# State-space output products: 128 stationary columns, one PSUM bank per head

## What is computed

```python
dt = softplus(dt_raw + dt_bias)
a_cum = cumsum(dt * -exp(a_log))                      # per head, along the tokens
xdt = xs * dt[..., None]                              # [token, head, 64]
decay = exp(where(causal, a_cum[l] - a_cum[s], -inf))
cb = einsum('ln,sn->ls', cm, bm)
y = einsum('ls,ls,sp->lp', cb, decay, xdt)            # sum over source tokens s
y = y + y_off                                         # chunks before, through a state
y = y + xs * d_skip
y = y * silu(z)
```

## Time and profile before

| what | value |
|---|---|
| median of 3 runs | 4614.47 us |
| the profiled execution | 4616.21 us, span 4614.4 us |
| PE busy | 4007.6 us (87%) |
| PEld busy | 3162.7 us (69%) |
| DVE busy | 2151.2 us (47%) |
| second block of `ssd` | about 206.3 to 345.7 us of the span |
| mean granted clock of PE | 0.893 |

### The profile page before, as it was taken

One profiled execution on the slowest core, in us unless ns is written; L12 is line 12 of the kernel. 1 busy time (PEld: TensorE's weight loads), 2 busy tenths in 40 slices (PEclk: granted clock), 3 DMA queues, 4 the chain that ended last, 5 costly groups with the idle time before them and its releaser, 6 DMA issues. The chain is left out here.

```text
span 4614.4 us, 53647 instructions
## 1 busy us (share of the span) xinstructions
PE 4007.6 (87%) x17473; PEld 3162.7 (69%) x17473; DVE 2151.2 (47%) x4054; ACT 1619.1 (35%) x2537; POOL 1620.4 (35%) x896
## 2 busy tenths in 40 slices
PE   7798758999659998998965988697799888999998
PEld 5436646877424566876764875576699888978886
DVE  1642173320233323311277113313498999378877
ACT  2322253322241223312245111322333688533333
POOL 3103233433210014433443431243267666633221
PEclk9759888999775579999988998898899999999999
DMA  2002102222100012222300231122257699799997
GB/s 89 29 0 87 62 14 80 94 92 72 45 29 0 0 37 91 94 88 65 93 14 19 91 96 32 55 91 68 97 174 250 221 336 332 286 357 361 344 343 246
DMA packets 275082, 573.61 MB, mean 124 GB/s; under 512 B 119777, under 2 KB 156001, under 8 KB 274545
## 3 DMA queue, kind: packets, MB, share of 16 engines
q1 hardware_dynamic: 238080, 437.71, 28.5%
q0 software_dynamic: 36864, 134.23, 8.6%
HBM read 517.33 MB, written 54.53 MB: 124 GB/s over the span
## 5 line engine op out<-in xcount | busy, mean ns | idle before, releaser
L382 PE MATMUL ps<-h_hi,w_hi 128*128 128x512 f32 x1868 | 740.7, 397 | 160.5 <-DVEq L510 73.9
L476 POOL TENSOR_TENSOR w_lo<-ring,w_hi 128x1024 fp32r<-128x1024 f32 (+3 forms) x193 | 462.7, 2398 | 1142.6 <-ACT w_hi L453 1142.6
L383 PE MATMUL ps<-h_lo,w_hi 128*128 128x512 f32 x1868 | 736.5, 394 | 0.0
L384 PE MATMUL ps<-h_hi,w_lo 128*128 128x512 f32 x1868 | 735.5, 394 | 0.0
L382 PEld LDWEIGHTS ps<-h_hi,w_hi 128*128 128x128 f32 x1868 | 356.9, 191 | 249.3 <-DVEq L510 63.7
L453 ACT CAST w_hi<-ring 128x1024 fp32r<-128x1024 f32 (+3 forms) x193 | 202.8, 1051 | 868.5 <-PE ps L384 807.5
L2208 PE MATMUL ps<-h_hi,w_hi 128*128 128x384 f32 (+1 forms) x1152 | 400.9, 348 | 22.9 <-PEq L208 21.6
L2035 ACT CAST w_hi<-ring 128x1024 fp32r<-128x1024 f32 x270 | 282.2, 1045 | 373.7 <-PE ps L384 281.0
L2160 POOL TENSOR_TENSOR w_lo<-ring,w_hi 128x1024 fp32r<-128x1024 f32 x142 | 358.0, 2525 | 152.6 <-ACT w_hi L2035 151.5
L384 PEld LDWEIGHTS ps<-h_hi,w_lo 128*128 128x128 f32 x1868 | 356.4, 191 | 75.9
L383 PEld LDWEIGHTS ps<-h_lo,w_hi 128*128 128x128 f32 x1868 | 357.0, 191 | 73.6
(11 more groups left out here) (365 smaller groups left out, 7773.3 us busy)
## 6 DMA issues: line engine op xcount, KB each, us to landing
ring<-in_expert_u SPq DMA_DIRECT2D x128, 512.0 KB, 4.8
ring<-in_expert_v SPq DMA_DIRECT2D x128, 512.0 KB, 5.7
ring<-in_w_gate_up SPq DMA_DIRECT2D x88, 512.0 KB, 3.7
acts<-expert_gelu SPq DMA_DIRECT2D x128, 192.0 KB
gates<-peer_region SPq DMA_DIRECT2D x48, 512.0 KB, 7.0
peer_region<-acts SPq DMA_DIRECT2D x128, 192.0 KB, 4.7
peer_region<-gates SPq DMA_DIRECT2D x128, 192.0 KB, 5.6
ring<-in_w_down SPq DMA_DIRECT2D x32, 704.0 KB, 4.0
```

What stands on the lines that cost most here:

```text
L382: pe.matmul(out, w_hi, x_hi, start=start, stop=False)
L383: pe.matmul(out, w_hi, x_lo, start=False, stop=False)
L384: return pe.matmul(out, w_lo, x_hi, start=False, stop=stop)
L476: pool.tensor_tensor(half(c.w_lo, s), raw(s), half(c.w_hi, s).bitcast(F32), ALU.subtract).then_inc(c.lo_done.sem, 1)
```

## The change

The output product of a head takes the 128 columns of its whole pair as the stationary operand (`xdt[:, j, 128 (h // 2) : ...]`). Its result has 128 partitions: 64 for its own head, and 64 of the other head's channels under this head's weights, which nobody reads. Each head now sums in a bank of its own, in turn 2, 3, 5, 6 (`sum_banks`). `pair(k)` reads the lower 64 partitions of the even head's bank and the upper 64 of the odd head's, with two instructions where one stood. `c_ready` counts two for a pair, and PE waits for it at the first step of every head from the fourth on, not of even heads only. Number and order of PE's products are the same.

```diff
-        banks = (0, 1, 4)
+        banks, sum_banks = (0, 1, 4), (2, 3, 5, 6)
...
-                    if j == 0 and h % 2 == 0 and h >= 4:
-                        pe.wait_ge(c.c_ready.sem, c.c_ready.at(h // 2 - 1))
+                    if j == 0 and h >= 4:
+                        pe.wait_ge(c.c_ready.sem, c.c_ready.at(2 * (h // 2 - 1)))
                     pe.wait_ge(c.b_ready.sem, c.b_ready.at(n + 1))
-                    p0 = 64 * (h % 2)
-                    mm = pe.matmul(c.ps[p0:p0 + 64, 2 + (h // 2) % 2, j * P:T], xdt[:, j, 64 * h:64 * h + 64],
+                    p0 = P * (h // 2)
+                    mm = pe.matmul(c.ps[:, sum_banks[h % 4], j * P:T], xdt[:, j, p0:p0 + P],
                                    M[:, n % 2, 0:T - j * P], start=j == 0, stop=j == NCH - 1)
...
                     dve.wait_ge(c.d_ready.sem, c.d_ready.at(2 * NCH * (k + 1)))
-                    dve.scalar_tensor_tensor(out[:, k, :], xs(k), c.col("d_skip", k),
-                                             c.ps[:, 2 + k % 2, :], ALU.mult, ALU.add).then_inc(c.c_ready.sem, 1)
-                    dve.wait_ge(c.c_ready.sem, c.c_ready.at(k + 1))
+                    at = COL_AT["d_skip"][0] + k
+                    for odd, rows in ((0, slice(0, 64)), (1, slice(64, P))):
+                        dve.scalar_tensor_tensor(out[rows, k, :], xbc[rows, k, :], c.cols[rows, at:at + 1],
+                                                 c.ps[rows, sum_banks[(2 * k + odd) % 4], :], ALU.mult, ALU.add
+                                                 ).then_inc(c.c_ready.sem, 1)
+                    dve.wait_ge(c.c_ready.sem, c.c_ready.at(2 * (k + 1)))
                     dve.tensor_tensor(out[:, k, :], out[:, k, :], z[:, k, :], ALU.mult).then_inc(c.dve_done.sem, 1)
...
-        c.c_ready.close(NH // 2)
+        c.c_ready.close(NH)
```

## The result

The changed kernel takes 4626.77 us in the median of 14 runs (4617.69 to 4631.69), the kernel before beside it 4614.26 us (14 runs, 4610.24 to 4621.75): 12.5 us slower by the medians. The ratio of the two, estimated from all runs, is 1.0025, 95% interval 1.0016 to 1.0033: 11.5 us, between 7 and 15. Forecast were 4623.7 us, 9.2 slower, in a range of 4615 to 4629. The profiled execution took 4631.7 us (span 4629.9).

The account below looks back on a forecast made before the run. PE at 1.2 GHz was taken to bound the block. Longer loads 6.7 us, DVE's pairs 1.9 and the last pair 0.65 sum to 9.2 us over the median of 4614.5: 4623.7 us, range 4615 to 4629.

Parts of the forecast that it names:

- The bound: Block of output products: PE, busy 132 of 134 us at clock 0.50 (1.2 GHz), sets its time.
- The load of 128 columns: Output product's stationary load, 128 columns for 64: 0.105 us more in each of 64 steps, 6.7 us, all on PE's path.
- rival 2: Load of 128 columns takes no longer than now, as with the transposes; only DVE's part remains, 3.4 us, 4617.9 us; chance 0.14.
- The pair: DVE's two instructions delay PE's j = 1 product by 0.29 us at seven pairs inside the block, taken as 1.9 us.
- the second costs 0.74 - 0.09 = 0.65 us: DVE's second pair instruction starts slightly before the first ends, so it adds 0.65 us to the first's 0.74.
- the end: Last pair, after PE's last product: nothing covers DVE's second instruction, so 0.65 us more.
- That half the partitions save nothing: DVE's pair instruction on 64 partitions takes as long as on 128, 0.74 us for the same 512 elements.
- The sum: Whole change: 6.7 + 1.9 + 0.65 = 9.2 us slower, 4623.7 us on the median.
- rival 3: DVE's halves cost more than one each, or pairs delay PE by the full 0.65: 12 us, 4626.4 us; chance 0.05.
- The clock: PE's clock in the block stays at 0.50, since the instructions of 16 rows remain between the output products.
- rival 1: 128 columns lift PE's clock to 1.00 soon after 210 us; a head takes 5.2 us, kernel 4560 (4546 to 4574); chance 0.11.
- Own banks and the odd heads' wait: A bank per head and odd heads waiting for `c_ready` cost nothing: banks are free and the pair was read long before.

Follow-up runs that it names:

- the runs with full rows: Spreading products take 128 rows, not 16: from the changed kernel 4569.75 us, from the kernel before 4573.70; with pair moved behind j = 2's weights 4575.56 and 4570.09.
- the first experiment: Changed kernel with output products back at 64 stationary columns, keeping a bank per head and two DVE instructions per pair: 4621.36 us against 4614.83, ratio 1.0014.

## Why the prediction was right, point by point

- **The bound.** PE at 1.2 GHz bounds the block, and nothing lies beside it. Right: what was added on PE came out in the block, but for two of the 64 loads.
- **The load of 128 columns.** Forecast 0.105 a step, 6.7 us. Between the starts of a product's two instructions 512 columns take 0.907 us before and 1.014 after: 0.107. It is on the path in 62 steps and not 64, 6.6 us: the last two products of the last head have their load covered. The two misses nearly cancel. By the rule of the Trainium skill, "TensorE: Matmul & The Clock Gate", section on LDWEIGHTS, 64 more columns are an estimate of 53 ns; the trace has twice that for these float32 products. The transposes' rows, my rival 2, were no guide: in the kernel before, two of them with 128 columns start 0.267 apart, as the output product's two instructions do with 64 (0.268); with 128 columns these start 0.375 apart. Why a transpose shows less of its load was not tried.
- **The pair.** The mechanism was right, in its place and its seven times, and the size was off. The failed term is "the second costs 0.74 - 0.09 = 0.65 us": I let the second half overlap the first as other DVE instructions do. It takes 0.78: L883's two last 1.51 to 1.52 together, and L887 follows 1.55 after their start where L884 came 0.77 after. So each pair inside holds PE up by 0.41 and not 0.29, 0.27 in the sum (starts 3.13 and 2.62 apart, less the 0.107 of the load), 2.9 us in place of 1.9, and the end costs 0.78 in place of 0.65. That half the partitions save nothing was right, 742 ns for 64 and 738 for 128.
- **The sum.** 6.6 + 2.9 + 0.8 = 10.3, as measured in the block; forecast were 9.2. The whole kernel's interval, 7 to 15 us, leaves out that nothing changed, but not that the change is under 9.2 us. That the median, 4626.77 us, lies on the 4626.4 of my rival 3 is chance: a pair holds PE up by 0.41 and not by the full 0.65, and the block gives 10.3 us and not 12.
- **The clock.** It didn't rise (rival 1), and for the reason given: the products of 16 rows. The prediction could only infer this from the end of the attention; the runs with full rows show it, since with nothing else changed in the block the clock is 1.00 at 64 columns as at 128. How many rows are enough was not tried. These runs came out at the upper edge of what I expected of a lifted clock (4569.8 and 4573.7 us in 4546 to 4574, with 4560 as the middle): a head takes 5.7 us with 128 columns and 5.55 with 64, where I had put 5.2.
- **Own banks and the odd heads' wait.** At nothing, as the first experiment shows.

## What to carry to other kernels

When a stretch runs at the low clock although PE never pauses, look at the rows of what runs between the large products: here a small product with a selector of 16 rows, padded with zeros to 128 at no cost in PE instructions, brought 38 to 45 us in four variants, while doubling the columns of the large product left the clock as it was and cost its load. Where products of different shapes took turns, the first load of each float32 product was on the path, and a wider stationary operand was paid for each time; where products of one shape followed each other, the load lay under the one ahead. That the shape decides is read from these rows and was not tried alone. Splitting the vector instruction by partitions doubled its time; move such work to a step where its engine waits, and count the last one in full, since nothing covers it.

## What was not expected of the hardware

From the kernel before to those with full rows the clock and the busy share of PE go opposite ways: 26.0 of 26 us busy at 0.50, 19.2 of 26 at 1.00. The Trainium skill, page "TensorE: Matmul & The Clock Gate", Part 1, lets the clock follow how busy PE has been; by that alone the kernel before would have had the full clock, and the runs disagree. Once the rows are full, pauses do go with falls of the clock, in the runs with 128 columns; whether they cause them was not tried.

Two DVE instructions on different halves of the partitions, with no semaphore between them, did not overlap at all: 1.51 us for two of 0.74, the second starting 0.03 us after the end of the first. It isn't that they are of the same kind. Elsewhere in the same trace two of that kind, both on all 128 partitions, take 1.41 us for two of 0.75:

```profile
22.19 1.41 DVE L357 SCALAR_TENSOR_TENSOR whole<-xT,cols_sb,rs 128x512 f32<-128x512 f32 x2 [5.78 <-ACT rs L317]
```

Of the DVE instructions in that trace that wait for no semaphore and follow closely, more than 1300 start before the end of the one ahead, and only these eight second halves after it. What sets them apart is that they begin at partition 64 behind one that begins at 0; no run tried it alone.
